# A two-layer attention and mixture-of-experts kernel: scatters in their own turn, last down-projections in half columns, first projections from raw rows, forget sums spread by a DMA

## The chip, the cores and the metric

The kernel runs on one core of one Trainium2 chip. The metric is the device time of one execution in microseconds (us); smaller is better. All data is float32. The engines are named as the profile names them: PE is TensorE's matmul pipe and PEld its weight load, DVE is VectorE, ACT is ScalarE, POOL is GpSimd and SP is SyncE, which here only issues DMAs. A "q" behind an engine's name is its instruction queue.

## The reference

256 tokens of width 1024 pass through two layers and a last norm. Cut to what matters:

```python
for l in range(2):
    h = rmsnorm(x, norm_attn[l])              # x * rsqrt(mean(x^2) + 1e-6) * gain
    proj = h @ w_in[l]                        # 1024 -> 6336: q, k, v of three attentions, gates, merge logits
    out_a = nsa_attention(...)                # 8 heads: compressed, selected and window branches
    c_q, c_kv = rmsnorm(mla_cq, ...), rmsnorm(mla_ckv, ...)
    out_b = causal_block_attention(q_b, k_b, v_b, ...)           # 8 heads with latent keys and values
    log_f = log_sigmoid(fox_f + fox_b_f[l])                      # 8 heads
    cum_log_f = cumsum(log_f, axis=1)                            # over the 256 tokens
    out_c = causal_block_attention(..., cum_log_f)               # score + cum[q] - cum[k]
    mixed = sum of sigmoid(merge + b) * (out @ w_o)              # three branches
    x = x + mixed @ w_out[l]
    t = rmsnorm(x, norm_ffn[l])
    # routing: one group of 4, two experts of its 8; then for each of 32 experts
    a, u = t @ w_gate[e], t @ w_up[e]                            # 1024 -> 256
    x = x + sum_e (silu(a) * u * weight[e]) @ w_down[e]          # 256 -> 1024
return rmsnorm(x, norm_final)
```

The expert weights are 32 x 3 MB in each layer, 201 MB over both. They are read once.

## The kernel before

**Memory.** `ring` is 20 slots of 1 MB in SBUF. In the attention stage slots 4, 5, 6, 7, 0, 1, ... (8 of them, `att_slot`) take the 36 loads of a layer's `w_in`, `w_uq`, `w_o` and `w_out`, and the other 12 MB (`region`) hold activations. In the expert stage all 20 slots take the 96 loads of the experts (`moe_slot`). `tail` holds what lives across both (`kept`). SP issues nearly all loads, in an order written out by hand, each behind a wait for the semaphore that says its slot is free. All engines run their own instruction lists with explicit semaphores.

**Attention stage.** Each of the two rows of 128 tokens is squared and summed (ACT L1037, DVE L1155), POOL works out 1/rms (`norm_pool`), DVE multiplies (L1161), PE turns h into `hT` by 16 transposes (L772), and DVE and ACT take it out of PSUM with the gain (L1166, L1044). In layer 0 PE runs `WARM` = 14 matmuls on the identity (`keep_warm`, L519) once the constants have landed, in layer 1 once the block begins. A float32 matmul is two instructions in the profile, a transpose one.

Then come 13 projections (`JOBS`; L_MPA is the first, L_MPB the second), each 16 matmuls of K = 128 against one 1 MB load: L841 (the first), L781 (`columns`) and L787 (`rows`). Between them lie the compression matmuls (L798), and in layer 0 the setup matmuls of the position bias (L569, L572). The job L_KS is the sixth, L_KW the seventh. After them follow the latent q, k and v (L875 to L892), compressed scores (L900), the transposes of the latent q (L910), and then the sums of the log forget gates: for each of 8 heads a column of `lf` is broadcast to 128 columns and multiplied with a triangle of ones (L930, L932), which leaves cum[k] on all 128 partitions; DVE multiplies by -8 and adds the causal mask into `bias8` and `bias0` (L1328, L1330). `gate_logits(0)` (L781 again) comes next, behind a wait for `s_mqte` 4, the four evictions of the latent q by ACT (L1101), then the compressed branch's output, then 16 units of attention, in which PE, DVE and ACT pass scores, probabilities and transposes to each other, and the merge (L1029).

**Expert stage.** w_out (L1485) adds into x, the tokens are routed, and experts are computed in 8 groups of 4, 32 token places each. In group g PE does: gate and up (L1579 in group 0, `gate_up`, L1557, in the others) behind the waits for its 8 loads; the gather of group g+1 (L1530); the transposes of the hidden rows (L1603), after ACT (L1678) and DVE (L1799, L1804); the scatter of group g-1 (`scatter`, L1564, 4 matmuls of 512 columns) into four PSUM banks; the transposes of the weighted selection (L1618); and the down matmuls (L1629), in two halves n = 0, 1 of 512 columns each, which ACT takes out (L1685). The last group's scatter follows behind the loop, and DVE adds the four banks to x (L1820).

SP's loads of the expert stage follow in `moe_sync`: load c of group g' = (c-20)//12 and place i waits for `s_g0` (group 0's gate and up), for `s_gu` g' (place 0: the slots of gate and up are free) and for `s_y` (place 8: those of down). The last four loads, c = 92 to 95, are the last group's downs, 1 MB each with 8 KB a partition. Behind them SP issues the first four loads of the next layer.

## Time and profile before

| | |
|---|---|
| time, median of 3 runs | 1103.22 us (1102.62 to 1103.24) |
| time of the profiled execution | 1102.17 us |
| its span on the core | 1100.2 us |
| PE busy | 970.0 us (88%), 5879 instructions |
| DVE, ACT, POOL busy | 274.2, 206.4, 24.7 us |
| mean granted TensorE clock | 0.95 |
| moved by DMA | 289.92 MB, mean 264 GB/s |

The span is what the profile covers; the 2.0 us between it and the execution's time lie around it. Busy time is a share of the whole, and the two layers each have a stage that PE fills and one that the weights' transfers fill, so that the mean says little; the rows below are read by stage.

### The profile page before, as it was taken

To read this page: it belongs to the slowest core of one execution; us is meant where nothing else is said; L and a number is where in the kernel's file an instruction comes from. 1 tells how busy PE (TensorE), PEld (TensorE's weight loads), DVE (VectorE), ACT (ScalarE), POOL (GpSimd) and SP (SyncE) were. 2 spreads that over 40 slices of the span, in tenths; PEclk is the share of its full clock that TensorE was granted. 3 is DMA by queue.
4 is the path that set the end of the run, shared out by engine and by line. 5 is a ranking of instruction groups with operands and counts; after the bars stand their busy time and mean duration, and the time that the engine had idled before them with its cause. 6 is when DMAs were issued, how large, how long until landed. Compare 5 with 4: busy or idle time off the path is not lost. (4 is left out here: it accounts for less than half of the span.)

```text
span 1100.2 us, 14272 instructions
## 1 busy us (share of the span) xinstructions
PE 970.0 (88%) x5879; PEld 694.0 (63%) x5879; DVE 274.2 (25%) x950; ACT 206.4 (19%) x561; POOL 24.7 (2%) x68
## 2 busy tenths in 40 slices
PE   7999999999999966777799999999999999666666
PEld 6898678778886333333289877887888854222222
DVE  2210433342423111110021214344333321000102
ACT  1211254441012100000011103444400300000001
POOL 0000000000000000000010000000000000000000
PEclk9999999999999988888899999999999999888888
DMA  9968233436946999999996342443398479999993
GB/s 287 284 152 266 78 103 127 158 111 231 365 169 232 420 422 421 420 422 421 364 251 228 117 152 59 133 136 132 115 332 317 154 309 421 422 420 423 421 422 123
DMA packets 122758, 289.92 MB, mean 264 GB/s; under 512 B 13390, under 2 KB 84164, under 8 KB 100164
## 3 DMA queue, kind: packets, MB, share of 16 engines
q1 hardware_dynamic: 119472, 286.25, 70.0%
q10 hardware_dynamic: 3220, 2.74, 1.5%
q8 instruction: 48, 0.79, 0.3%
q14 instruction: 18, 0.15, 0.0%
HBM read 286.35 MB, written 2.62 MB: 263 GB/s over the span
## 5 line engine op out<-in xcount | busy, mean ns | idle before, releaser
L781 PE MATMUL bank<-tail,ring 128*128 128x256 f32 x1280 | 288.8, 381 | 0.0
L781 PEld LDWEIGHTS bank<-tail,ring 128*128 128x128 f32 x1280 | 239.3, 190 | 38.9 <-issue 8.3
L1557 PE MATMUL bank<-ring,tail 128*32 128x512 f32 x896 | 123.6, 713 | 100.1 <-DMA ring<-in_moe_w_up 100.1
L1557 PEld LDWEIGHTS bank<-ring,tail 128*32 128x32 f32 x896 | 34.4, 128 | 188.9 <-issue 188.9
L1799 DVE SCALAR_TENSOR_TENSOR tail<-tail,bank 128x256 f32<-128x256 f32 x16 | 6.7, 422 | 318.2 <-ACT tail L1678 318.2
L1029 PE MATMUL bank<-tail,ring 128*128 128x256 f32 x384 | 83.4, 380 | 0.0
L1029 PEld LDWEIGHTS bank<-tail,ring 128*128 128x128 f32 x384 | 72.8, 190 | 10.2 <-issue 0.3
L1119 ACT ACTIVATE ring<-ring,small 128x128 f32<-128x128 f32 (+1 forms) x128 | 56.6, 443 | 77.5 <-DVE small L1362 77.5
L1530 PEld LDWEIGHTS bank<-tail 128*128 128x128 f32 x512 | 58.5, 192 | 12.9 <-issue 12.2
L1530 PE MATMUL bank<-tail 128*128 128x128 f32 x512 | 61.9, 278 | 0.8 <-DVE tail L1737 0.5
L1629 PE MATMUL bank<-ring,tail 128*32 128x512 f32 x512 | 58.2, 595 | 0.6 <-DVE tail L1810 0.6
L1564 PE MATMUL bank<-tail 128*128 128x512 f32 x128 | 57.8, 594 | 0.0
L1485 PE MATMUL bank<-ring,tail 128*128 128x256 f32 x256 | 56.7, 380 | 0.0
L787 PE MATMUL bank<-ring,tail 128*128 128x256 f32 (+2 forms) x320 | 53.7, 327 | 0.0
L1485 PEld LDWEIGHTS bank<-ring,tail 128*128 128x128 f32 x256 | 48.2, 190 | 6.3
L787 PEld LDWEIGHTS bank<-ring,tail 128*128 128x128 f32 x320 | 49.7, 191 | 3.6
L1678 ACT ACTIVATE tail<-bank 128x256 f32<-128x256 f32 x16 | 6.1, 384 | 237.9 <-PE bank L1557 214.9
L1355 DVE CUSTOM_DVE_ANT_0 ring<-bank,ring 128x128 f32<-128x128 f32 x96 | 28.6, 354 | 62.7 <-PE bank L971 62.7
L1564 PEld LDWEIGHTS bank<-tail 128*128 128x128 f32 x128 | 23.2, 191 | 24.6 <-issue 24.6
L1629 PEld LDWEIGHTS bank<-ring,tail 128*32 128x32 f32 x512 | 15.0, 109 | 32.1 <-issue 31.1
L971 PE MATMUL bank<-ring 64*128 64x128 f32 (+3 forms) x256 | 34.8, 347 | 0.0
L1377 DVE TENSOR_TENSOR ring<-ring,small 128x256 f32<-128x256 f32 x64 | 32.9, 555 | 1.1
(253 smaller groups left out, 777.2 us busy)
## 6 DMA issues: line engine op xcount, KB each, us to landing
ring<-in_moe_w_gate SPq DMA_DIRECT2D x64, 1024.0 KB, 26.2
ring<-in_moe_w_up SPq DMA_DIRECT2D x64, 1024.0 KB, 26.4
ring<-in_moe_w_down SPq DMA_DIRECT2D x64, 1024.0 KB, 23.3
ring<-in_w_in SPq DMA_DIRECT2D x48, 1024.0 KB, 7.4
ring<-in_w_out SPq DMA_DIRECT2D x8, 1024.0 KB, 10.4
ring<-in_w_o_mla SPq DMA_DIRECT2D x4, 1024.0 KB, 5.1
ring<-in_w_o_fox SPq DMA_DIRECT2D x4, 1024.0 KB, 5.0
ring<-in_w_o_nsa SPq DMA_DIRECT2D x4, 1024.0 KB, 5.4
```

The costliest lines, as they stand in the source:

```text
L781: last = pe.matmul(dst, weight(k), hT[:, k, :], start=(k == 0), stop=(k == KD - 1))
L787: last = pe.matmul(dst, hT[:, k, t * P:(t + 1) * P], weight(k), start=(k == 0), stop=(k == KD - 1))
L971: last = pe.matmul(bank[half][:, lo:hi], q[:, t * P:(t + 1) * P], k[:, 0:hi - lo], start=True, stop=True)
L1029: last = pe.matmul(bank[q % 4][:, 0:T], wo[:, c, (m % 4) * P:(m % 4 + 1) * P], oT[:, b, c, :], start=(c == 0), stop=(c == 3))
L1119: last = act.activation(pr, pr, ACT.Exp, scale=scale, bias=mx[:, c:c + 1], accum_out=sm[:, c:c + 1])
L1355: last = dve.tensor_tensor_reduce(out=prob[u % 3][:, half, lo:hi], in0=bank[half][:, lo:hi], in1=b, scale=1.0, scalar=PAD, op0=ALU.add, op ...
L1377: last = dve.tensor_tensor(pr, pr, bc(factors(rs, u)[:, t, :], [P, 2, hi - lo]), ALU.mult)
L1485: last = pe.matmul(bank[4 + i][:, t * T:(t + 1) * T], mixT[:, k, t * P:(t + 1) * P], w[:, k, :], start=(k == 0), stop=(k == KD - 1))
L1530: last = pe.matmul(b[:, (k % 4) * P:(k % 4 + 1) * P], h2[:, t, k, :], Sel[:, g % 2, t, :], start=(t == 0 and k % 4 == 0), stop=(t == NT - ...
L1557: last = pe.matmul(bank[4][CAP * e:CAP * e + CAP, :].rearrange("p (a f) -> p a f", a=2), XT[:, g % 2, k, CAP * e:CAP * e + CAP], ring[:, l ...
L1564: return pe.matmul(bank[2 * t + half][:, :], ST[:, g % 2, t * P:(t + 1) * P], ysb[:, 512 * half:512 * half + 512], start=(g == 0), stop=(g ...
L1629: last = pe.matmul(bank[5 + n][CAP * e:CAP * e + CAP, :], hidT[:, a, CAP * e:CAP * e + CAP], ring[:, moe_slot(12 * g + 8 + e), a * D + 512 ...
```

## The change

Four parts, in the words of the code:

1. **First projections from raw rows.** PE transposes x itself (not h); the gain goes in on the way out of PSUM (`xT`), the sum of squares comes after it on ACT and DVE. The jobs L_MPA and L_MPB multiply xT, and 1/rms is applied when their result is taken out. Behind L_MPA PE spreads 1/rms over all partitions (two matmuls with the identity into bank 7, `s_rb`), and DVE multiplies xT by it into `hT` (four instructions of 128x512, `s_hn`), for which the job L_NQ waits. The 14 warm-ups of layer 1 go; those of layer 0 run on zeros as soon as they are set. The constants are loaded in two parts, the identity first. The bias matmuls of layer 0 move behind L_MPB.
2. **Forget sums.** Behind L_KS one matmul pair computes the sums of the 8 heads as 8 rows of 256; DVE scales them (`crow`), SP stores them to HBM (8 KB) and, behind load 16, reads them back onto all 128 partitions into `bias8` (1 MB written). DVE adds the mask in two instructions (128x8x128 and 128x8x256) behind `s_kcT`. L930, L932, L1328 and L1330 go.
3. **Own-turn scatter.** Every group scatters behind its own downs. In the last group the transposes of the selection come ahead of those of the hidden rows.
4. **The last downs** are loaded in 8 transfers of 0.5 MB (2 KB rows): the left halves of the four, then the right ones, for which n = 1 waits (`s_late`). In the last group 12 warm-ups (`TAILWARM`) stand ahead of the waits for the last two loads of gate and up.

Some semaphores are merged, and the branch for overflowing experts, which isn't taken here, counts PE's steps in one.

```diff
+TAILWARM = 12
+    def down_half(sp, layer, c, n, done):
+        g, i = divmod(c, 12)
+        src = A["moe_w_down"][layer, 4 * g + GROUP[i][0]].rearrange("(p j) n -> p j n", j=2)
+        slot = ring[:, moe_slot(c), :].rearrange("p (j n) -> p j n", j=2)
+        sp.dma_start(slot[:, :, 512 * n:512 * n + 512], src[:, :, 512 * n:512 * n + 512]).then_inc(done, 16)
...
     def setup_tensor(pe):
+        pe.wait_ge(u_ms, 1)
+        for _ in range(WARM):
+            pe.matmul(bank[7][:, 0:P], zeros, zeros, start=True, stop=True)
+        pe.wait_ge(u_id, 32)
+        pe.transpose(bank[5][:, 0:16], stage[0:16, :], ident[0:16, 0:16]).then_inc(u_prep, 1)
...
                 attention_load(sp, layer, n)
+                if n == RING + L_KW:
+                    sp.wait_ge(s_cr, 1)
+                    sp.dma_start(cum_rows[layer], crow).then_inc(s_cs, 16)
+                if n == RING + L_FQ + 1:
+                    sp.wait_ge(s_cs, 16)
+                    sp.wait_ge(s_hc, 1)
+                    sp.dma_start(bias8, cum_rows[layer].partition_broadcast(P)).then_inc(s_cb, 16)
...
         def attention_tensor(pe):
-            if layer:
-                keep_warm(pe, WARM, bank[7])
-            for t in range(NT):
-                pe.wait_ge(s_h, t + 1)
-                for k in range(KD):
-                    last = pe.transpose(bank[k // 2][...], hA[:, t, k * P:(k + 1) * P], ident)
+            if layer == 0:
+                pe.wait_ge(u_x, 16 * NT)
+            for r in range(4):
+                for j in range(2):
+                    for t in range(NT):
+                        last = pe.transpose(bank[r][:, j * T + t * P:j * T + t * P + P],
+                                            x[:, t, (2 * r + j) * P:(2 * r + j + 1) * P], ident)
+                last.then_inc(s_ht, 1)
...
                     last.then_inc(s_proj, 1)
                     if layer == 0:
-                        setup_bias_tensor(pe)
+                        setup_columns_tensor(pe)
+                    pe.wait_ge(s_rstd, 1)
+                    for t in range(NT):
+                        last = pe.matmul(bank[7][:, t * P:(t + 1) * P], rstd[:, t:t + 1].broadcast_to([P, P]), ident,
+                                         start=True, stop=True)
+                    last.then_inc(s_rb, 1)
                     continue
+                if n == L_NQ:
+                    pe.wait_ge(s_hn, 4)
...
+                if n == L_MPB and layer == 0:
+                    setup_bias_tensor(pe)
+                if n == L_KS:
+                    pe.wait_ge(s_lf, 1)
+                    pe.matmul(bank[7][0:H, 0:T], lf[:, 0, :], cst[:, K_TRI:K_TRI + T], ...)
+                    pe.matmul(bank[7][0:H, P:T], lf[:, 1, :], cst[:, K_TRI:K_TRI + P], ...).then_inc(s_fb, 1)
...
             pe.wait_ge(s_mve, 2)
-            pe.wait_ge(s_lf, 1)
-            for i in range(4):
-                (two heads each: lf column broadcast x triangle, L930 and L932)
             pe.wait_ge(s_mqte, 4)
             gate_logits(0)
...
+            dve.wait_ge(s_rb, 1)
+            for r in range(4):
+                dve.tensor_tensor(hT[:, 2 * r:2 * r + 2, :], xT[:, 2 * r:2 * r + 2, :],
+                                  bank[7][:, 0:T].unsqueeze(1).broadcast_to([P, 2, T]), ALU.mult).then_inc(s_hn, 1)
...
+            dve.wait_ge(s_cb, 16)
+            dve.tensor_tensor(bias0, bias8[:, :, 0:P], mask[:, :, P:T], ALU.add).then_inc(s_fbe, 1)
+            dve.wait_ge(s_fbe, 1)
+            dve.tensor_tensor(bias8, bias8, mask, ALU.add).then_inc(s_fbe, 1)
             take(12, fv[:, :, 256:512], two(bank[0]))
...
+            sp.wait_ge(s_gu, NGRP - 2)
+            for c in range(LOADS - 4, LOADS):
+                down_half(sp, layer, c, 0, landed[moe_slot(c)])
+            for c in range(LOADS - 4, LOADS):
+                down_half(sp, layer, c, 1, s_late)
...
                 for i in range(8):
+                    if g == NGRP - 1 and i == 6:
+                        keep_warm(pe, TAILWARM, bank[5])
                     moe_wait(pe, 12 * g + i)
...
-                if g:
-                    pe.wait_ge(s_ste, g)
-                    pe.wait_ge(s_ye, 2 * g)
-                    for half in range(2):
-                        for t in range(NT):
-                            last = scatter(g - 1, t, half)
-                    last.then_inc(s_scat, 1)
...
+                    if n == 1 and g == NGRP - 1:
+                        pe.wait_ge(s_late, (layer + 1) * 64)
...
+                pe.wait_ge(s_ste, g + 1)
+                for half in range(2):
+                    pe.wait_ge(s_ye, 2 * g + half + 1)
+                    for t in range(NT):
+                        last = scatter(g, t, half)
+                        if g == NGRP - 1:
+                            last.then_inc(s_fin, 1)
+                if g < NGRP - 1:
+                    last.then_inc(s_scat, 1)
```

## Rows read from the trace of the kernel before

**Rows 1.** The page, part 2: DMA in 40 slices of 27.5 us.

```profile
DMA  9968233436946999999996342443398479999993
GB/s 287 284 152 266 78 103 127 158 111 231 365 169 232 420 422 421 420 422 421 364 251 228 117 152 59 133 136 132 115 332 317 154 309 421 422 420 423 421 422 123
```

**Rows 2.** Who PE waited for, whole span: total us, times, longest us.

```profile
PE bank L1557 <- DMA ring<-in_moe_w_up: 100.1, 12, 10.5
```

**Rows 3.** Windows: busy by engine, granted clock, DMA share, GB/s.

```profile
344.00:346.00 2.00, 2.00 (x20) 0.73 (x24) 1.05 (x5) 0.00 (x0) 0.04 (x1) 1.00 0.00 0
...
1078.00:1079.00 1.00, 0.11 (x4) 0.00 (x0) 0.41 (x1) 0.38 (x1) 0.00 (x0) 1.00 0.48 197
```

**Rows 4.** Timeline, first 60 us: start, length, what, [idle before].

```profile
5.80 6.16 PE L519 MATMUL bank<-cst 128*128 128x128 f32 x28 [5.80 <-DMA cst<-in_shape_c]
...
7.31 1.23 DVE L1155 CUSTOM_DVE_ANT_0 ring<-x_res 128x1024 f32<-128x1024 f32 x1 [7.31 <-DMA x_res<-in_x]
...
13.33 1.97 PE L772 MATMUL bank<-cst,ring 128*128 128x128 f32 x16 [1.25 <-DVE ring L1161]
...
15.59 7.15 PE L841 MATMUL bank<-ring,tail 128*128 128x256 f32 x32 [0.30 <-DVE tail L1166]
...
25.00 5.45 PE L787 MATMUL bank<-ring,tail 128*128 128x192 f32 x32
...
30.28 24.34 PE L781 MATMUL bank<-tail,ring 128*128 128x256 f32 x112
```

**Rows 5.** DMA issues at 1.6 us and from 48 to 60: KB, us to landing.

```profile
ring<-in_w_in SPq DMA_DIRECT2D x1, 1024.0 KB, 8.6
...
ring<-in_w_in SPq DMA_DIRECT2D x1, 1024.0 KB, 34.9
```

**Rows 6.** Timeline, start of layer 1.

```profile
552.77 3.39 PE L519 MATMUL bank<-cst 128*128 128x128 f32 x28 [1.62 <-PEq L1823]
...
558.15 7.14 PE L841 MATMUL bank<-ring,tail 128*128 128x256 f32 x32 [0.22 <-DVE tail L1166]
```

**Rows 7.** Timeline, forget sums and the first gate logits, layer 0.

```profile
125.92 1.95 PE L910 MATMUL bank<-cst,ring 128*96 128x128 f32 x16
...
127.80 2.03 ACT L1101 ACTIVATE ring<-bank 96x512 f32<-96x512 f32 x4
...
129.70 0.68 DVE L1328 SCALAR_TENSOR_TENSOR ring<-bank,cst 128x512 f32<-128x512 f32 x1
...
133.49 3.62 PE L781 MATMUL bank<-tail,ring 128*128 128x256 f32 x16
```

**Rows 8.** Part 6 of the page: median us from issue to landing.

```profile
ring<-bias_table SPq DMA_DIRECT2D x2, 1024.0 KB, 5.6
```

**Rows 9.** Timeline, first turns of the expert stage, layer 0, PE and SP.

```profile
359.00 7.05 PE L1557 MATMUL bank<-ring,tail 128*32 128x512 f32 x64
...
366.11 1.76 SPq L499 DMA_DIRECT2D ring<-in_moe_w_down  x4
...
369.89 3.60 PE L1564 MATMUL bank<-tail 128*128 128x512 f32 x8
...
379.54 8.77 PE L1557 MATMUL bank<-ring,tail 128*32 128x512 f32 x64 [2.27 <-DMA ring<-in_moe_w_up]
```

**Rows 10.** Timeline, last group of either layer (528.79: layer 0).

```profile
528.79 9.58 PE L1557 MATMUL bank<-ring,tail 128*32 128x512 f32 x64 [9.46 <-DMA ring<-in_moe_w_up]
...
1068.95 9.15 PE L1557 MATMUL bank<-ring,tail 128*32 128x512 f32 x64 [9.87 <-DMA ring<-in_moe_w_up]
...
1079.52 0.50 PE L1603 MATMUL bank<-cst,tail 128*128 128x128 f32 x2 [1.41 <-DVE tail L1804]
...
1083.60 3.64 PE L1629 MATMUL bank<-ring,tail 128*32 128x512 f32 x32
```

**Rows 11.** Window in the last group of layer 1: TensorE's granted clock rises.

```profile
1073.00:1073.50 0.50, 0.50 (x8) 0.14 (x4) 0.00 (x0) 0.00 (x0) 0.00 (x0) 0.81 0.97 410
```

**Rows 12.** Window of DMA alone, layer 0: expert loads with rows of 2 KB.

```profile
276.00:278.00 2.00, 1.00 1.05 386
```

More of the change, by code:

```diff
@@ L182, in program @@
     hT = kept(0, KD, T)
+    xT = kept(2048, KD, T)
     mixT = kept(2048, KD, T)
@@ L200, in program @@
     hA = region(2048, NT, D)
+    zeros = region(2048, P)
     mqT = region(2048, H, T)
@@ L359, in program @@
     s_fb = csem("cum_forget_psum")
+    s_cr = csem("cum_forget_rows_taken")
+    s_cs = csem("cum_forget_rows_stored")
+    s_cb = csem("cum_forget_spread")
     s_fbe = csem("cum_forget_taken")
@@ L556, in setup_gpsimd @@
         pool.memset(rexp, -0.5)
+        pool.memset(zeros, 0.0).then_inc(u_ms, 1)
         pool.memset(rbd, 0.0)
@@ L1035, in attention_scalar @@
             if layer == 0:
-                act.wait_ge(u_x, 16 * NT)
+                act.wait_ge(u_cols, 1)
+            for r in (1, 3):
+                act.wait_ge(s_ht, r + 1)
+                for j in range(2):
+                    last = act.activation(xT[:, 2 * r + j, :], bank[r][:, j * T:(j + 1) * T], ACT.Copy,
+                                          scale=g_att[:, layer, 2 * r + j:2 * r + j + 1])
+                last.then_inc(s_xTa, 1)
             act.activation(hA[:, 0, :], x[:, 0, :], ACT.Square, accum_out=ss[:, 0:1]).then_inc(s_ss, 1)
@@ L1039, in attention_scalar @@
                 setup_loads(act)
-                act.wait_ge(u_cols, 2)
-            for r in (1, 3):
-                act.wait_ge(s_ht, r + 1)
-                for j in range(2):
-                    last = act.activation(hT[:, 2 * r + j, :], bank[r][:, j * T:(j + 1) * T], ACT.Copy,
-                                          scale=g_att[:, layer, 2 * r + j:2 * r + j + 1])
-                last.then_inc(s_hTa, 1)
             def take(n, dst, src):
@@ L1050, in take @@
                 act.activation(dst, src, ACT.Copy).then_inc(s_eva, 1)
-            take(1, mp[:, :, 256:448], two(bank[1])[:, :, 0:192])
+            act.wait_ge(s_proj, L_MPB + 1)
+            act.wait_ge(s_rstd, 1)
+            for t in range(NT):
+                last = act.activation(mp[:, t, 256:448], two(bank[1])[:, t, 0:192], ACT.Copy, scale=rstd[:, t:t + 1])
+            last.then_inc(s_eva, 1)
             act.wait_ge(s_evd, 1)
@@ L1153, in attention_vector @@
             if layer == 0:
-                dve.wait_ge(u_x, 16 * NT)
+                setup_gains_vector(dve)
+            for r in (0, 2):
+                dve.wait_ge(s_ht, r + 1)
+                dve.tensor_tensor(xT[:, 2 * r:2 * r + 2, :], two(bank[r]),
+                                  bc(g_att[:, layer, 2 * r:2 * r + 2], [P, 2, T]), ALU.mult).then_inc(s_xTd, 1)
             dve.tensor_tensor_reduce(out=hA[:, 1, :], in0=x[:, 1, :], in1=x[:, 1, :], scale=1.0, scalar=0.0,
@@ L1178, in take @@
                 dve.tensor_copy(dst, src).then_inc(s_evd, 1)
-            take(0, mp[:, :, 0:256], two(bank[0]))
+            dve.wait_ge(s_proj, L_MPA + 1)
+            dve.wait_ge(s_rstd, 1)
+            for t in range(NT):
+                last = dve.tensor_scalar(mp[:, t, 0:256], two(bank[0])[:, t, :], rstd[:, t:t + 1], None, ALU.mult)
+            last.then_inc(s_evd, 1)
             take(2, nqT[:, 0:2, :], two(bank[2]))
@@ L1431, in moe_sync @@
             load_overflow(sp)
-            for c in range(SLOTS, LOADS):
+            for c in range(SLOTS, LOADS - 4):
                 g, i = divmod(c - SLOTS, 12)
```

171 lines of the change are left out of this document (78 added, 93 removed).

## The prediction

> **What bounds the kernel now.** I read the page's 40 slices first. DMA's digits [rows 1] show two plateaus of nines, one in each layer's expert stage, with gaps between them. In the list of who PE waited for, one wait is large, 100.1 us in 12 pieces, for the transfers of gate and up [rows 2]; no other wait of PE for data is over 6 us. So there are two regimes. Where the digits are low, PE fills the time, and every us taken off PE's chain moves all that follows. On a plateau the weights' transfers fill it, and PE's work counts only behind the last transfer. The windows show where one turns into the other: at 344 to 346 nothing is moved while PE works without a gap, so the plateau begins when PE frees the first slots; it ends at 1078 to 1079, with the last downs [rows 3]. Its length is 76 MB at one rate and isn't touched. What is saved ahead of it shifts it, what is saved behind it is saved, and what is saved inside is waited away.
>
> **Start of layer 0.** PE's first projection starts at 15.6 [rows 4]. The constants land at 5.8, x at 7.3, and the 1 MB of the first projection's weights 8.6 us after its issue at 1.6, so at 10.2 [rows 4, 5]. In the changed kernel the warm-ups (6.2 us) need only zeros and run from about 1.1 to 7.3; the transposes of x then take 2.0 us, and the first quarter of xT is out of PSUM about 1 us after x is there. So the weights come last, at 10.2: 5.4 us earlier. Behind it PE now has a transpose and the spreading of 1/rms, four instructions of 0.12 us (the pitch of L519 in [rows 6]), 1.0 us with its gaps. The bias matmuls, which hold the gap from 22.7 to 25.0 [rows 4], move behind the second projection and cost the same 2.3 us there. 10.2 + 7.15 + 1.0 + 5.3 + 2.3 = 26.0, against 30.3 for the third projection [rows 4]: **4.3 us** saved. If the weights land as much as 0.8 earlier, since most of the constants now come behind them, it is 5.1; if 0.8 later, 3.5. DVE's four multiplications of 128x512 (0.68 each [rows 7]) are hidden beside the second projection's 5.3 us; without that cover they would cost 2.7.
>
> **Start of layer 1.** PE starts at 552.8 either way, at the block's start. Transposes of x take 1.9 or 2.0 [rows 4], so the first projection starts at 554.7 and not at 558.15 [rows 6]: 3.5. The squares, 1.3 us on each engine, and POOL's rsqrt now have the 7.1 us of that projection as cover. The spreading costs 0.6 here: **2.9 us** saved.
>
> **The clock there.** The 28 warm-up instructions of 3.39 us [rows 6] went at full clock. Without them the stretch from the last scatter (its end is 1.62 us ahead of 552.77 [rows 6]) to 554.7 holds 3.5 us in which PE does transposes only. After an idle time of 2.27 us a gate and up matmul set took 8.77 us where the same set takes 7.05 at full clock [rows 9]; after 9.5 to 9.9 us it took 9.58 and 9.15 [rows 10]. So a fall to half costs 1.7 to 2.5, and no fall costs 0. No row shows whether transposes hold the clock. By length, 3.5 is nearer to the gap of 2.27 that lost it than to the gap of 1.62 that kept it, so I take the fall, **2.1 us** lost. The Trainium skill (TensorE: Matmul & The Clock Gate, Part 4: PE-mode transpose) says that the full rate does not engage for transposes; by that page the loss comes, and if the page doesn't hold here the sum is 2.1 better.
>
> **Forget sums.** The old part starts behind the transposes that end at 127.9, and `gate_logits(0)` comes at 133.5 [rows 7]. Without it PE would go on at once, but that step waits for the fourth eviction by ACT, which ends at 127.80 + 2.03 = 129.83 [rows 7]. So 3.5 are saved and not 5.6, in each layer: **7.0 us**. PE stands idle for 2.0 there; if that drops the clock, it costs 1.7 each [rows 9]. The 8-row form costs PE two instructions of 256 columns (0.22 each, L841 in [rows 4]) and two of 128 (0.12, L519 in [rows 6]) behind L_KS, 0.7 with rounding: **1.3 us** lost over both layers. Its wait for `s_lf` should be free: DVE's last steps for lf hang on the job before, and L_KS gives them some 7 us of PE's work as cover; if lf came that late again, the wait would be PE's. The rest is off the path if the spread lands in time. It is issued behind load 16, at some 80 us, and 1 MB of the same form took 5.6 us from issue to landing [rows 8]; DVE asks for it at about 95 and needs 3.5 us for the mask (0.68 for 512 columns [rows 7]), and the next in its queue, the eviction of the thirteenth job, is due only at 108. On SP the waits for `s_cr` and `s_cs` stand ahead of loads 15 and 17, which the merge gates need after 129.
>
> **Own-turn scatters.** A scatter is 3.6 us of PE [rows 9]. In groups 2 to 6 PE has nearly 10 us of waiting to put it in [rows 2]. In group 0 and 1 it comes ahead of the next gate and up. The loads that wait for group 1's gate and up go out at 366.1 now [rows 9], would go out at 370, and at that time 8 MB issued before last until 377: the queue doesn't run dry. Cost 0; bound from the other side, 3.6 if it did. In the last group the scatter, the selection's transposes and the bubbles lie between 1079.5 and 1083.6 on the path [rows 10]; without them the downs start 1.0 after the transposes of the hidden rows (0.50, then DVE's copy), so 3.1 are saved in each layer: **6.2 us**.
>
> **Warm-ups in the last group.** Its gate and up take 9.58 and 9.15 [rows 10] against 7.05 [rows 9], since PE comes out of an idle time at half clock. The clock rose 4.2 us after work began at 1068.95 [rows 10, 11]. The warm-ups start when six of eight loads are there, 5.0 us ahead of the last (2 MB at 422 GB/s [rows 1]), and 24 instructions of 0.22 [rows 4] last 5.3 at half clock. So they fill the wait, the clock rises about when the last load is there, and I take 7.4 for the set: 2.2 and 1.75, **3.9 us** saved. Bounds: the 28 warm-ups at the program's start went at half clock for all their 6.2 us [rows 4], and if that happens here 0.3 is lost for the overrun and about 1.5 gained each; nothing at all is the floor.
>
> **Half columns.** The last downs used to be there at about 1078.5 [rows 3], and PE asked at 1083.6. Now it asks for the left halves at 1078.3 and for the right ones at 1080.0. The left ones are there 5 us earlier than the right; 2 KB rows moved at 386 GB/s [rows 12] and the plateau's 8 KB rows at 422 [rows 1], so 4.2 MB take 10.9 us and not 9.9, and the right halves land near 1079.5. Cost 0, bound 1.
>
> **Sum.** -4.3 - 2.9 + 2.1 - 7.0 + 1.3 - 6.2 - 3.9 = -20.9. The profiled execution took 1102.2 (span 1100.2 and 2.0 around it) and lies 1.0 under the median of the three runs. 1102.2 - 20.9 = 1081.3, with the 1.0 on top **1082.3**; its own range, from the terms' bounds, is 1080.5 to 1085. Under 0.2% (2.2 us) this kernel's measurement can't be told from no change.
>
> **Rivals.**
> - *The clock holds* through the transposes of layer 1: 1080.2. For it: only 1.62 us are wholly idle [rows 6]. Chance 0.25.
> - *The ends don't shorten as planned*: the clock rises late and the right halves land late. 3.9 and 1.0 come back: 1087.2. For it: the cold start of 6.2 us [rows 4]. Against it: 4.2 us at 1068.95. Chance 0.18.
> - *The first 4.3 us are waited for again.* In layer 0 a load issued at 48 landed 34.9 us later [rows 5], at 82.7, and its job now starts at 93.5 and not 98. The store of the bias table fills DMA then. If the loads slip with it by more than 10 us, PE waits in the tenth to twelfth job: 1086.6. Chance 0.09.
> - *Slower: the spread of the forget sums is late.* The 8 KB store is queued behind that same table store, SP waits for it to land before it issues the spread, and DVE stands behind the spread with the evictions that PE's latent q waits for. The store goes out at about 82; at 34.9 us each [rows 5] the spread lands at 152, and PE, which wants its thirteenth job evicted at 108, waits 48 us: 1130. It decides the sign when the spread lands after 125 in layer 0. Against it: by 80 the table's store has nearly drained, and a table read of the spread's size took 5.6 [rows 8]. The Trainium skill (DMA: Bandwidth & Descriptors, the section on why a DMA increments its semaphore by 16) says that a transfer with 8 rows outermost runs on 8 engines at most; by that page the new 8-row store and the table's store, which also has 8 outermost, share their engines. The 34.9 us [rows 5] agree with such a jam, but no row of them shows which engines it holds. Chance 0.03.
>
> **Chances.** The forecast has 0.43, the rivals 0.25, 0.18, 0.09 and 0.03; 0.02 is left for more than all this. 1078 to 1088 takes in all but the slow case and some of the unknown. Faster 0.96, same 0.01, slower 0.03.
>
> **What would show it.** In the changed kernel's profile: the first projection at 10 and its successor L_NQ at 26; in layer 1 the first projection 1.9 us behind the block's first transpose, with a granted clock of 0.5 in part of it if the fall is right; PE idle for 2 us ahead of the first gate logits and nothing there from L_KS's four instructions; the plateau of layer 0 starting at about 337 and not 347; in the last groups a gate and up set of 7.4 us and downs 2.4 us behind its end. A wait of PE on DVE in the thirteenth job, of DVE on the spread, or a DMA share under 0.9 inside a plateau would each make it wrong.

## Result and the profile after

The changed kernel takes **1090.88 us** (median of 4 runs, 1086.04 to 1092.14) and the kernel before 1102.92 (4 runs, 1102.22 to 1103.24): ratio 0.9889, 95% interval 0.9874 to 0.9905. It is faster by 12 us where 20.9 were forecast, and lies 8.6 us above the forecast and 2.9 outside its range. The same kernel, run again beside the first experiments, took 1087.69 (1087.25 to 1091.72), ratio 0.9878 [0.9865, 0.9892]: 14.4 us faster than the kernel before, and just inside the range. The profiled execution took 1092.14, span 1090.3, the longest of the four.

The page of the changed kernel, part 2 in 40 slices of 27.3 us (PE clock in tenths, DMA in tenths, GB/s):

```profile
PEclk9999999999999998888899999999999999888888
DMA  9879333436945999999997542443398479999994
GB/s 301 198 173 346 96 104 129 156 115 215 368 188 191 422 422 421 420 421 422 367 314 237 166 143 78 138 144 117 105 348 308 154 309 422 421 421 420 422 415 158
```

The two plateaus are still there [rows 1]. Timeline of PE in layer 0, from the first projection to the first gate logits (start, length, what, idle time before):

```profile
9.29 7.17 PE L879 MATMUL bank<-ring,tail 128*128 128x256 f32 x32 [0.96 <-DMA ring<-in_w_in]
...
24.48 24.42 PE L819 MATMUL bank<-tail,ring 128*128 128x256 f32 x112
...
52.40 0.60 PE L909 MATMUL bank<-cst,small 128*8 128x256 f32 x2
...
75.67 15.77 PE L819 MATMUL bank<-tail,ring 128*128 128x256 f32 x64 [3.34 <-DMA ring<-in_w_in]
...
98.63 13.98 PE L825 MATMUL bank<-ring,tail 128*128 128x256 f32 x64
...
126.24 1.95 PE L962 MATMUL bank<-cst,ring 128*96 128x128 f32 x16
130.24 5.38 PE L819 MATMUL bank<-tail,ring 128*128 128x256 f32 x16 [2.05 <-issue]
```

The third projection starts at 24.48 and not at 30.28 [rows 4]: 5.8 us gained. At 75.67 PE waits 3.34 us for a load, and the set behind it takes 15.77 us, 14.08 at full clock (77.04 in the kernel before). At 126.24 the transposes of the latent queries start 0.3 us *later* than before [rows 7]. So the whole start of layer 0 is lost by then. The first gate logits follow behind 2.05 us of idle time, at half clock: 5.38 us, 3.62 before [rows 7].

Why a load is late stands in the queues. SP and ACT in the kernel before, then in the changed one:

```profile
42.99 33.60 SPq L462 DMA_DIRECT2D ring<-in_w_in  x5
...
45.17 0.79 ACTq L629 DMA_DIRECT2D bias_table<-ring  x1
```

```profile
39.45 0.80 ACTq L660 DMA_DIRECT2D bias_table<-ring  x1
...
42.00 5.21 SPq L724 DMA_DIRECT2D tail<-in_moe_w_router  x1
47.25 31.26 SPq L471 DMA_DIRECT2D ring<-in_w_in  x5
```

The store of the bias table used to go out 2.2 us behind the first of SP's five loads; it comes 5.7 us earlier with the whole start, while SP's small loads ahead of `w_in` come only about 1 us earlier, and so it is now ahead of the five. Issues of the five loads, two of them in the kernel before (at 42.99 and 45.85) and the first in the changed one (KB, us to landing):

```profile
ring<-in_w_in SPq DMA_DIRECT2D x1, 1024.0 KB, 8.3
...
ring<-in_w_in SPq DMA_DIRECT2D x1, 1024.0 KB, 33.6
```

```profile
ring<-in_w_in SPq DMA_DIRECT2D x1, 1024.0 KB, 28.4
```

So the store held up loads in the kernel before as well: SP took 33.6 us to issue the five, and the third landed at 79.4. But the first, for which the ninth projection waits, had landed at 51.3, and the others were not yet wanted. Behind the store the first one lands at 75.6.

Layer 1's start, the last groups of both layers (528.8 and 1069 in [rows 10]), PE:

```profile
524.20 5.46 PE L535 MATMUL bank<-cst 128*128 128x128 f32 x24 [4.32 <-DMA ring<-in_moe_w_up]
529.59 7.23 PE L1608 MATMUL bank<-ring,tail 128*32 128x512 f32 x64
...
539.26 3.64 PE L1676 MATMUL bank<-ring,tail 128*32 128x512 f32 x32 [0.52 <-DVE tail L1861]
542.83 3.70 PE L1615 MATMUL bank<-tail 128*128 128x512 f32 x8
548.16 1.97 PE L811 MATMUL bank<-cst,x_res 128*128 128x128 f32 x16 [1.63 <-PEq L1874]
549.96 7.07 PE L879 MATMUL bank<-ring,tail 128*128 128x256 f32 x32
...
1062.37 7.08 PE L1608 MATMUL bank<-ring,tail 128*32 128x512 f32 x64
...
1071.89 5.34 PE L1676 MATMUL bank<-ring,tail 128*32 128x512 f32 x32 [0.52 <-DVE tail L1861]
1077.16 3.70 PE L1615 MATMUL bank<-tail 128*128 128x512 f32 x8
```

The downs start 2.4 us behind the end of gate and up in both layers, as forecast; in layer 1 they run at half clock (5.34 us for 3.64). In layer 1 the first projection takes 7.07 us: the clock did not fall in the transposes (granted clock 1.00 from 546 to 550).

The first gather in the routing, PE in layer 0, in the kernel before and in the changed one:

```profile
337.29 2.02 PE L1530 MATMUL bank<-tail 128*128 128x128 f32 x16 [0.15 <-ACT tail L1662]
```

```profile
335.81 3.45 PE L1579 MATMUL bank<-tail 128*128 128x128 f32 x16
```

It runs at a granted clock of 0.50 from 336 to 338, and in layer 1 it takes 3.24 us. A wait for VectorE behind it (0.64 us before) takes up part of this, so that it costs some 0.5 us in each layer.

**Where the spans differ.** Each stage ends where the next begins: the first gate and up (343.95 before), the last load of gate and up, the end of its matmuls, the end of the last scatters. The last load lands 4.93 us behind the start of the warm-ups (in the mended kernel's trace 516.18 to 521.11, where PE still waits behind them), so at 529.1 and 1061.9 here. In us against the kernel before; the last column is an experiment's (f1):

| stage | forecast | changed | mended (f1) |
|---|---|---|---|
| attention and routing, layer 0 | -7.15 | -1.0 | -7.9 |
| plateau, layer 0 (184.8 us) | 0 | +1.3 | +0.2 |
| last gate and up (9.58) | -2.2 | -1.9 | -2.5 |
| last downs and scatters (12.8) | -3.1 | -3.1 | -3.1 |
| attention and routing, layer 1 | -3.65 | -3.6 | -5.8 |
| plateau, layer 1 (185.0) | 0 | +1.2 | 0 |
| last gate and up (9.15) | -1.75 | -1.6 | -2.1 |
| last downs and scatters (12.8) | -3.1 | -1.4 | -3.1 |
| end | 0 | +0.1 | 0 |
| sum | -20.9 | -9.9 | -24.1 |

Of the 11.0 us between forecast and changed kernel some 4.0 were lost ahead of the transposes at 126.24, 3.4 in the gate logits of both layers, 1.0 in the gathers, 2.5 in the plateaus, 1.7 in layer 1's last downs and 0.5 at the last gate and up; some 2.4 came back at layer 1's start.

### The profile page after: what moved, and what is told of

It is laid out like the page before. It is cut to its first block and busy times, and to the rows that moved or that the text cites. A ratio compares the mean times of both kernels' runs of the same rounds, so it can differ in the third digit from the quotient of the medians.

```text
span 1090.3 us, 14225 instructions
## 1 busy us (share of the span) xinstructions
PE 975.8 (89%) x5852; PEld 696.0 (64%) x5852; DVE 277.1 (25%) x947; ACT 207.3 (19%) x564; POOL 24.8 (2%) x69
## 5 line engine op out<-in xcount | busy, mean ns | idle before, releaser
L819 PE MATMUL bank<-tail,ring 128*128 128x256 f32 x1280 | 294.3, 386 | 7.4 <-issue 4.1
L819 PEld LDWEIGHTS bank<-tail,ring 128*128 128x128 f32 x1280 | 242.8, 193 | 48.8 <-issue 13.3
L1608 PE MATMUL bank<-ring,tail 128*32 128x512 f32 x896 | 117.4, 683 | 71.7 <-DMA ring<-in_moe_w_up 71.7
L1068 PE MATMUL bank<-tail,ring 128*128 128x256 f32 x384 | 83.4, 380 | 0.0
L1068 PEld LDWEIGHTS bank<-tail,ring 128*128 128x128 f32 x384 | 72.8, 190 | 10.2 <-issue 0.3
L1579 PEld LDWEIGHTS bank<-tail 128*128 128x128 f32 x512 | 61.2, 199 | 12.6 <-issue 11.9
L1579 PE MATMUL bank<-tail 128*128 128x128 f32 x512 | 64.5, 286 | 0.5 <-DVE tail L1788 0.5
L1676 PE MATMUL bank<-ring,tail 128*32 128x512 f32 x512 | 59.9, 610 | 5.2 <-DVE tail L1861 5.2
L1615 PEld LDWEIGHTS bank<-tail 128*128 128x128 f32 x128 | 23.0, 189 | 36.4 <-issue 36.4
```

Of the source, the lines that this page charges most:

```text
L819: last = pe.matmul(dst, weight(k), hT[:, k, :], start=(k == 0), stop=(k == KD - 1))
L1068: last = pe.matmul(bank[q % 4][:, 0:T], wo[:, c, (m % 4) * P:(m % 4 + 1) * P], oT[:, b, c, :], start=(c == 0), stop=(c == 3))
L1579: last = pe.matmul(b[:, (k % 4) * P:(k % 4 + 1) * P], h2[:, t, k, :], Sel[:, g % 2, t, :], start=(t == 0 and k % 4 == 0), stop=(t == NT - ...
L1608: last = pe.matmul(bank[4][CAP * e:CAP * e + CAP, :].rearrange("p (a f) -> p a f", a=2), XT[:, g % 2, k, CAP * e:CAP * e + CAP], ring[:, l ...
L1615: return pe.matmul(bank[2 * t + half][:, :], ST[:, g % 2, t * P:(t + 1) * P], ysb[:, 512 * half:512 * half + 512], start=(g == 0), stop=(g ...
L1676: last = pe.matmul(bank[5 + n][CAP * e:CAP * e + CAP, :], hidT[:, a, CAP * e:CAP * e + CAP], ring[:, moe_slot(12 * g + 8 + e), a * D + 512 ...
```

## The experiments

Medians are of 4 to 6 runs, each kernel timed beside the kernel before (1101.3 to 1102.1). "The unchanged one" is the changed kernel as it is, at 1087.69. It was timed with the result (1090.88) and with the runs whose names begin with e, not with those of f, g and h; its nine runs together have a median of 1088.9. A difference between a kernel of f, g or h and 1087.69 is therefore uncertain by some 3 us, and counts as shown only where rows of the traces bear it out.

> The changed kernel once more, beside the others of its batch. Its four runs so far lay between 1086.0 and 1092.1, median 1090.9. If the spread comes from where the clock falls, runs with a higher mean granted clock are the shorter ones, and the median stays at 1088 to 1092. If it came from the chip of the first batch, all runs lie close together at another level.

Measured: 1087.69.

**The late load.** The store is moved on ACT's queue behind the eighth take.

```diff
-        act.wait_ge(u_cp, 1)          # in setup_trig_scalar
-        act.dma_start(table, tabs.unsqueeze(1).broadcast_to([H, P, OH_W])).then_inc(u_tb, 16)
+            if layer == 0:            # in attention_scalar, behind take(7, ...)
+                act.wait_ge(u_cp, 1)
+                act.dma_start(table, tabs.unsqueeze(1).broadcast_to([H, P, OH_W])).then_inc(u_tb, 16)
```

> The changed kernel with the store of the bias table moved on ACT from its place behind the log forget gates (39.5 us) to behind the seventh projection's eviction (about 67 us). Theory A (the store, now issued 5.7 us earlier, goes ahead of the projections' loads 8 to 12 and takes back the start's gain in layer 0): PE does not wait for w_in at 75.7, the last projection ends about 5 us earlier, the time falls by 4 to 5.5 us. Rival (the loads are late for their own sake, because DMA is full at the start whatever ACT stores): the wait of 3.3 us at the ninth projection stays and the time moves by less than 1 us. If the new 8 KB store or the spread now meets the table's store, DVE waits for the spread longer than the 1.9 us of the changed kernel.

Measured: 1083.04 (1081.04 to 1085.7), ratio 0.9822 [0.981, 0.9835], 4.65 less. Windows from 44 to 52 us of the changed kernel and of this one (busy of each engine, clock, DMA share, GB/s):

```profile
44.00:52.00 8.00, 8.00 (x53) 7.43 (x52) 2.13 (x7) 0.00 (x0) 0.00 (x0) 1.00 0.51 74
```

```profile
44.00:52.00 8.00, 8.00 (x52) 7.38 (x51) 2.13 (x7) 0.00 (x0) 0.72 (x1) 1.00 1.04 326
```

With the store in the queue half of the DMA time is used and 74 GB/s moved; without it 326. Its timeline (PE, SP, DVE):

```profile
72.55 14.08 PE L817 MATMUL bank<-tail,ring 128*128 128x256 f32 x64
...
109.76 7.09 PE L926 MATMUL bank<-ring 128*128 128x384 f32 x16 [1.96 <-DVE ring L1222]
...
80.24 5.24 SPq L743 DMA_DIRECT2D ring<-cum_rows  x1
...
105.46 1.22 DVE L1324 TENSOR_TENSOR ring<-ring,cst 128x1024 f32<-128x1024 f32 x1 [10.05 <-DMA ring<-cum_rows]
```

The wait and the cold set are gone, and the first gate and up of layer 0 starts at 339.45, 4.0 us earlier than in the unchanged kernel of the same set of runs (343.44). But the store now stands ahead of the spread of the forget sums: VectorE waits 10.05 us for it and PE 1.96 us for VectorE, and then works at half clock. This is the slow rival of the prediction in small.

**Why the store holds the queue.** The same 1.5 MB, but 128 rows outermost instead of 8, by way of a 12 KB copy to HBM. That changes two more things: the source is now HBM and no longer 8 partitions of SBUF, and the store goes out at 42.66, 0.4 us behind the first of the five loads, not at 39.45.

```diff
-        act.dma_start(table, tabs.unsqueeze(1).broadcast_to([H, P, OH_W])).then_inc(u_tb, 16)
+        act.dma_start(rows8, tabs).then_inc(u_t8, 16)
...
+        act.wait_ge(u_t8, 16)         # behind the angles
+        act.dma_start(table.rearrange("h p w -> p h w"), rows8.unsqueeze(0).broadcast_to([P, H, OH_W])).then_inc(u_tb, 16)
```

> The changed kernel with the table's store in two steps from the same place: the eight rows first as 12 KB, then the 1.5 MB from there with 128 rows outermost instead of 8. If the store is slow because eight rows outermost keep it on half of the engines, it now lasts some 5 to 10 us instead of 30, SP's five loads behind it are issued in about 9 us as with the late store, TensorE waits for nothing at the ninth projection, and the time is that of the late store or a little less: 1083, 1081.5 to 1084.5. If it is the store itself, whatever its shape, the loads land as late as before and the time stays at 1087.7, within 1.

Measured: 1080.29 (1078.3 to 1083.03), ratio 0.9806 [0.9793, 0.9819]. Its timeline of SP, PE and DVE, then a window and the DMA issue (KB, us to landing):

```profile
42.29 14.29 SPq L473 DMA_DIRECT2D ring<-in_w_in  x5
...
72.81 14.08 PE L823 MATMUL bank<-tail,ring 128*128 128x256 f32 x64
...
95.59 1.22 DVE L1327 TENSOR_TENSOR ring<-ring,cst 128x1024 f32<-128x1024 f32 x1
```

```profile
44.00:52.00 8.00, 8.00 (x51) 7.35 (x50) 2.13 (x7) 0.00 (x0) 0.72 (x1) 1.00 1.01 304
...
bias_table<-bias_rows ACTq DMA_DIRECT2D x1, 1536.0 KB, 10.4
```

The store lands in 10.4 us, the five loads go out in 14.3 us and not 31.3, and neither PE at 72.8 nor VectorE at 95.6 waits. So it is not a matter of 1.5 MB being stored there. Nor is it the place: in the kernel before the narrow store went out 2.2 us behind the first load, and the five still took 33.6 us to issue. What is left is the shape and the source together; no run changes one alone. The Trainium skill (DMA: Bandwidth & Descriptors, the section on why a DMA increments its semaphore by 16) says that a transfer with 8 rows outermost runs on at most 8 of the 16 engines; the share of 0.51 with 8 rows and of 1.01 with 128 agree with it. Which engines these are no view shows. But half of the engines is not all. The store's queue from 74 to 79 us in the run with the late store, where next to nothing else was moved, and from 43 to 53 with the wide store (packets, MB, share of 16 engines):

```profile
q10 hardware_dynamic: 167, 0.26, 44.5%
```

```profile
q10 hardware_dynamic: 1040, 1.57, 47.6%
```

A packet of 1.5 KB took 213 ns of one engine's time there and 73 here (0.445 x 5 us x 16 / 167, and 0.476 x 10 us x 16 / 1040). So the narrow store was slow by a factor of 2 from the engines that it left idle and of 2.9 from the time of each packet, and the second factor, for which the source is a candidate, stays unexplained.

**The gap of the forget sums.**

```diff
             pe.wait_ge(s_mve, 2)
+            keep_warm(pe, 8, bank[4])
             pe.wait_ge(s_mqte, 4)
```

> The changed kernel with 8 warm-up matmuls (16 instructions) in the gap where the forget sums were, ahead of the wait for the latent q's evictions. Theory B (the 2.05 us of idle PE let the clock fall, and the first gate logits take 5.4 us and not 3.6 in both layers): the logits take 3.6 us, the time falls by 3 to 3.6 us. Rival (the clock falls there by chance, and the run-to-run spread hides it): under 1.5 us on the median.

Measured: 1084.11 (1082.34 to 1085.57), ratio 0.9832 [0.982, 0.9845], 3.6 less. The logits run at full clock in both layers; layer 0:

```profile
129.52 1.95 PE L535 MATMUL bank<-cst 128*128 128x128 f32 x16
131.69 3.72 PE L819 MATMUL bank<-tail,ring 128*128 128x256 f32 x16 [0.22 <-ACT ring L1144]
```

In the unchanged kernel's trace of the same set of runs only one of the two logits was at half clock (1.7 us). The rest of the 3.6 lies elsewhere: both its gathers were at half clock and here none is, and its plateau and last gate and up of layer 1 are longer. That the filler is worth 3.6 is not shown.

**The parts undone, one by one.** First the forget sums as before: the four loops of sixteen matmuls behind the wait for `s_mve`, their eight evictions on VectorE, no rows of eight, no store, no spread.

> The changed kernel with the forget sums as before: sixteen matmuls behind the latent query transposes, taken by VectorE with the mask, no rows of eight, no store, no spread. What the part brings is then the difference to the unchanged one (1087.7). The forecast's size: 7.0 less 1.3 is 5.7 us, 1093.4. By the traces since: 3.5 us in each layer, less 0.75 each for the rows of eight, less 1.7 in the layers where the gate logits run at half clock behind the 2.05 us gap (one of two in that profile): 3.8 us, 1091.5, between 1090 and 1092.5. That the part brings nothing (the rival): 1087.7.

Measured: 1090.99 (1090.21 to 1091.69), ratio 0.9904 [0.9889, 0.992]: 3.3 over 1087.69, but the same as the unchanged one's first median, so that the medians alone say anything from 0 to 3.3. The rows say more. Attention and routing of layer 1 take 329.6 us with the old sums and 327.1 with the new ones where nothing falls to half clock (e1), so the part brings 2.5 us in a layer; in the changed kernel's profile, with logits and gather at half clock, it is 329.2, and next to nothing is left.

Then the scatter order of before (`scatter(g - 1, t, half)` behind the hidden transposes, the last group's at the end; one wait for `s_ye` ahead of the warm-ups, which keeps their bank free).

> The changed kernel with the scatter of a group behind the next group's gate and up, and that of the last group at the end, as before; halves and warm-ups stay. The forecast's size of the own-turn scatter, 3.1 us in each layer: 1087.7 + 6.2 = 1093.9, between 1092.5 and 1095. The rival: the old order leaves TensorE no stops in the last group (the scatters stand where it now waits 1.05 and 0.52 us), the downs are never at half clock, and the part is worth less, 4 to 5 us: 1092.

Measured: 1093.85 (1089.67 to 1097.84), ratio 0.9929 [0.9908, 0.995]: 6.2 over 1087.69, as the forecast had it, and by the rows 3.07 in each layer (from the end of the last gate and up to the end of the scatters 12.77 us here and 9.70 with the own turn). Its plateaus are as long as the mended kernel's (start of the first gate and up to the last load: 185.1 and 185.0 for 185.0 and 185.0), so the own-turn order costs nothing inside.

Whole downs instead of halves (the four loads back in the loop, no `s_late`):

> The last group's four down matrices are loaded whole again, with no second wait. The forecast's step (the halves cost and bring nothing, bound 1 us): 1087.7, within 0.7. The rival: the own-turn scatter brings the last downs forward to 9.7 us behind the start of the last gate and up, while four whole loads of 1 MB take some 10 us at 410 GB/s behind the last up; then the downs wait 0.5 to 2 us in each layer without the halves, and the time is 1089 to 1091.

Measured: 1089.54 (1088.46 to 1090.64), ratio 0.9885 [0.987, 0.99], which overlaps the unchanged one's. In its profile the downs wait 0.56 and 0.52 us for VectorE and never for a load. So the halves bring nothing that this measurement shows.

**The warm-ups.** `TAILWARM = 0` and `TAILWARM = 8`:

> The changed kernel without the 12 warm-ups of the last groups. Theory C (the warm-ups begin 3.7 us ahead of the last load, last 5.46 us, so they hold the set up for 1.7 us and win about 2.1 by the clock: little is left): the set starts 1.7 us earlier in each layer and takes 8.7 to 9.6 us; the time rises by 0 to 2 us. Forecast's theory (they win 2 us in each layer): the time rises by 3.5 to 4 us. If they cost more than they bring, it falls.

Measured: 1093.82 (1090.6 to 1097.35), ratio 0.9928 [0.9912, 0.9945], 6.1 more. Its last gate and up of layer 0:

```profile
529.90 8.47 PE L1608 MATMUL bank<-ring,tail 128*32 128x512 f32 x64 [8.32 <-DMA ring<-in_moe_w_up]
```

In layer 1 they take 8.41. From the landing of the last load to the end of gate and up it is 8.7 us in both layers, and 7.8 and 7.6 in the changed kernel's profile, 7.2 and 8.0 in the unchanged one's of this set: the stage shows 2.0 to 2.2 us over both layers, which is about what theory C gives. The median shows 6.1. So the runs do not settle theory C, and what lies between 2.2 and 6.1 is not shown to be the warm-ups'.

> TAILWARM = 8 alone. Theory C2: the twelve warm-ups start on a cold engine and last 5.46 us, 1.7 us longer than the 3.7 us that are left to the last load, and so eat the gain that they bring; eight last some 3.4 us, the last gate and up start when the load lands and take about 7.1 us: 1 to 1.5 us less in each layer, 1085.5 us (1084.5 to 1086.5). The rival, that eight are too few: the gate and up take some 8.4 us again as without warm-ups, and the time lies between 1088.5 and 1094.

Measured: 1090.23 (1087.45 to 1093.68), ratio 0.9887 [0.9868, 0.9906]: no better than 1087.69. In layer 0 they leave a stop of 1.72 us and gate and up take 9.98 us:

```profile
524.18 3.21 PE L535 MATMUL bank<-cst 128*128 128x128 f32 x16 [3.48 <-DMA ring<-in_moe_w_up]
529.11 9.98 PE L1608 MATMUL bank<-ring,tail 128*32 128x512 f32 x64 [1.72 <-issue]
```

The last load lands 4.93 us behind the start of the warm-ups, so the wait to be filled is 4.9 us and not the 3.7 that this expectation had; twelve that start at half clock overrun it by 0.5 us.

> Four warm-ups behind the last group's selection transposes, where TensorE waits 1.05 us for VectorE's hidden rows. Theory: the downs of the last group ran at half clock (5.34 us for 3.64) in layer 1 of two profiles out of four because of the two short stops of 1.05 and 0.52 us ahead of them; filled, they are never cold, and the median falls by 0.5 to 1.5 us: 1086.5. The rival: it was the warm-ups' own overrun or chance, and nothing moves: 1087.7 within 0.7.

Measured: 1087.04 (1084.61 to 1088.89), ratio 0.9864 [0.9849, 0.9879]. Its downs take 3.64 and 3.65 us, but the median cannot be told from the unchanged one's.

**All together:** the late store, the gap filled, `TAILWARM = 8`, and on VectorE the two additions of the mask behind the last take.

```diff
-            dve.wait_ge(s_cb, 16)
-            dve.tensor_tensor(bias0, bias8[:, :, 0:P], mask[:, :, P:T], ALU.add).then_inc(s_fbe, 1)
...
             take(12, fv[:, :, 256:512], two(bank[0]))
+            dve.wait_ge(s_cb, 16)
+            dve.tensor_tensor(bias0, bias8[:, :, 0:P], mask[:, :, P:T], ALU.add).then_inc(s_fbe, 1)
...
```

> Four edits together on the changed kernel: the table's store behind the eighth take of ScalarE; eight warm-ups of TensorE in the 2.0 us gap that the forget sums leave; the two additions of the mask on VectorE behind its last take, so that they no longer stand in front of it when the spread lands late (in the run with the late store alone VectorE waited 10.05 us for the spread and TensorE 1.96 us for VectorE); and eight warm-ups instead of twelve ahead of the last gate and up. If the losses are separate, as the runs so far say, the gains add: 4.6 + 3.6 + 1.1, and 0.5 to 2 for the shorter warm-ups, from 1087.7: 1077.5 us, between 1075.5 and 1079.5. The rival: what one edit fills lets the clock fall elsewhere (the routing's gather, the last downs), and the sum stops near 1081.

Measured: **1077.92** (1077.13 to 1083.69), ratio 0.9787 [0.9764, 0.981], 9.8 under the unchanged one and 24 under the kernel before. Its timeline of PE:

```profile
72.68 14.08 PE L817 MATMUL bank<-tail,ring 128*128 128x256 f32 x64
...
108.81 5.40 PE L926 MATMUL bank<-ring 128*128 128x384 f32 x16 [0.88 <-DVE ring L1223]
...
125.53 3.72 PE L817 MATMUL bank<-tail,ring 128*128 128x256 f32 x16 [0.22 <-ACT ring L1145]
...
336.09 7.07 PE L1632 MATMUL bank<-ring,tail 128*32 128x512 f32 x64 [0.62 <-DVE tail L1837]
```

All three losses of layer 0 are gone, and its first gate and up starts 7.9 us earlier than in the kernel before. The medians' gains, 4.65 and 3.6, leave 1.5 for the other two edits, but this sum does not say which edit brought what: from the late store alone to this kernel the first logits move from 128.22 to 125.53, both at full clock, so the mask's place brings 2.7 us by itself.

> The mended kernel (late store, gap filled, mask behind the last take) with twelve warm-ups instead of eight ahead of the last gate and up. In the mended kernel's profile the eight begin 3.9 us ahead of the last load and leave a stop of 1.3 us behind them, and gate and up run at full clock, 7.07 us. Alone, eight gave 1090.2 for the twelve's 1087.7. If twelve fill the stop and start at full clock (4.5 us) they overrun by nothing or 0.7 us: 1077 to 1079.5, no difference from the 1077.9 of the eight. If the twelve start on a cold engine (5.46 us) they overrun by 1.6 us in each layer: 1080 to 1081.

Measured: 1078.95 (1078.28 to 1081.23), ratio 0.9798 [0.9783, 0.9812]. The medians of eight and twelve can't be told apart. The profiles can: with twelve the last gate and up take 7.07 to 7.44 us in all 20 places of the ten profiles that have them; eight leave a stop of 1.2 to 1.7 us, and in three of eight places gate and up then start cold (9.98 above, 9.22 and 9.17 in h2 and h3). Twelve are the safer choice.

> The mended kernel with no warm-ups ahead of the last gate and up. By the rows of the run without warm-ups (8.4 us for 7.07 in each layer) they bring 2.7 us: 1080.6. By that run's median (6.1 us over the unchanged one) they bring more than their own matmuls: 1083 to 1084.5. By the forecast's size, 3.9: 1081.8.

Measured: 1085.58 (1084.24 to 1085.9), ratio 0.9854 [0.9839, 0.9869], 7.7 more. Its last gate and up, where the mended kernel takes 7.07 twice:

```profile
521.11 9.46 PE L1610 MATMUL bank<-ring,tail 128*32 128x512 f32 x64 [9.02 <-DMA ring<-in_moe_w_up]
...
1054.14 9.19 PE L1610 MATMUL bank<-ring,tail 128*32 128x512 f32 x64 [9.27 <-DMA ring<-in_moe_w_up]
```

These two rows are 4.5 us of the 6.4 between the two profiles' spans. Another 1.2 are a longer plateau in layer 1, and 0.6 lie in its attention and routing, where a gather ran at half clock; both lie ahead of that layer's warm-ups. So between these two profiles the warm-ups are worth some 4.5 us, a little over the forecast's 3.9 and twice what the run without them alone showed, and what the two medians show beyond that is not shown to be theirs.

> The wide store, the gap filled and eight warm-ups in the last groups, but no edit to the mask's place, since nothing delays the spread then. With the theory of the engines it equals the mended kernel, 1078, within 1. If the store's shape is not the cause, it is the run with the gap filled alone, 1084.

Measured: 1082.8 (1079.12 to 1083.39), ratio 0.9809 [0.9793, 0.9825]: it can't be told from the wide store alone, and 1078 was expected. The logits are at full clock as meant, but in this profile three gathers (3.02, 3.58 and 3.37 us for 2.02, 2.05 and 2.02) and the last gate and up of layer 1 (9.22) are not. In the wide store's own profile the gap was unfilled, and the clock held in both layers.

> The mended kernel once more, on the chip of this call: 1077.9, within 1.5.

Measured: 1080.13 (1078.53 to 1081.09), ratio 0.9795 [0.9782, 0.9809]. Both times the mended kernel lies under every median of the kernel before and of the changed one; the wide store alone (0.9806) can't be told from it. Here its last gate and up of layer 0 start cold:

```profile
521.00 9.17 PE L1610 MATMUL bank<-ring,tail 128*32 128x512 f32 x64 [1.20 <-issue]
```

## Why the prediction was wrong

- **Start of layer 0** failed. At the third projection 5.8 us had come where 4.3 were forecast; at the ninth 5.0 went, 3.34 in the wait and 1.7 at half clock, and the rows of eight took 0.75. That is the rival "The first 4.3 us are waited for again", which had 0.09 and nearly the right price, but placed the wait in the tenth to twelfth job and had the loads slip by some 10 us. Its row was at hand, 34.9 us from issue to landing [rows 5], and the prediction took it for a delay that all the loads have. What decides is which loads stand behind the store: in the kernel before the first of the five, the ninth projection's, was ahead of it and landed at 51.3; in the changed one it is behind it and lands at 75.6. The store passed it because the earlier start pulled ACT's issue forward by 5.7 us and SP's by about 1; that step was costed for PE alone, not for what ACT issues with it. The late store gave back 4.65 by the median. By the start of layer 0's first gate and up it is 4.0: 5.0 at the load and 1.7 by gate logits that stayed at full clock, less 2.7 lost at the spread. The wide store has this start at 336.24, 7.2 earlier, of which 2.2 are logits and a gather that stayed at full clock.
- **Forget sums** were mis-sized: 5.7 forecast; by the rows 5.1 where no clock falls (2.5 in a layer, g1 beside e1), and each fall takes 1.7 from it. At 9 falls in 18 places that is an estimate of 3.4, and g1's median gave 0 to 3.3. The 2.0 us gap lies where it was put (2.05), and the clause "if that drops the clock, it costs 1.7 each" should have been in the sum with its chance: the logits took 5.38 us and not 3.7 in 9 of 18 places of this kind, over the nine profiles that have the gap and no filler. The rows of eight cost 0.75 each for 0.65.
- **The clock there** failed in the other direction. In all 16 profiles with the new start, the changed kernel's and the experiments', layer 1's first projection takes 7.07 us behind a stop of 1.59 to 1.64. The Trainium skill (TensorE: Matmul & The Clock Gate, Part 4: PE-mode transpose), by which the full rate does not engage for transposes, does not hold for this stretch; the measurement decides. The start of layer 1 gained 3.2 where 2.9 less 2.1 were forecast.
- **Own-turn scatters** were right: -3.1 in layer 0's last group, and 3.07 in each by g2's rows; nothing was lost inside the plateaus. What was not foreseen is that the downs, now behind two short stops of 1.05 and 0.52 us, can run at half clock: +1.7 in layer 1 of this profile, and in 4 of the 28 places of the profiles that have both stops unfilled. Nor were the routing's gathers: the first one is at half clock in 20 of 32 layers of the new profiles and in neither of the kernel before, some 0.5 us each; what lets its clock fall is open.
- **Warm-ups** were right in the mechanism, and nearly in size against the kernel before: 1.9 and 1.6 in the changed kernel for 2.2 and 1.75; up to 2.5 and 2.1 where they start at full clock. Against the same kernel without them it is 2.0 to 2.2 in one pair of profiles (e3) and 4.5 in another (g4).
- **Half columns**: nothing, as said.
- **The slow rival** did not happen in the changed kernel (VectorE waits 1.9 us for the spread, off the path), but the late store called it up: 10.05 us. It needed the table's store ahead of the spread (67.69 and 80.24).
- Not foreseen at all: a plateau of 186.1 and 186.2 us for 184.8 and 185.0, 2.5 us. Part of it goes in the first 12 us, where the windows of the changed kernel show

```profile
347.00:355.00 8.00, 7.70 (x72) 5.00 (x65) 2.43 (x5) 0.77 (x2) 0.57 (x2) 1.00 0.99 390
880.00:888.00 8.00, 7.70 (x72) 5.13 (x68) 2.67 (x6) 0.77 (x2) 0.76 (x2) 1.00 1.00 408
```

against 420 and 419 GB/s in the same place of the kernel before, at the same DMA share: 8 us x 30 / 421 = 0.6 us and 0.2 us. Both layers of e1 and f3 have it too, and no layer of e2, f1, g1, g2 and g3. The same kernel's second profile (e0) has a plateau as short as before in layer 0 and a long one in layer 1, so it differs between executions of one kernel, and is not shown to come from the change. Its cause stays open.

Open too is where the clock falls from run to run. The changed kernel's runs spread over 6 us, those of before over 1 to 3, and two profiles of it differ in such places (the logits of layer 1 took 5.36 us in one and 3.69 in the other, its last downs 5.34 and 3.74). With the gap filled h2 shows falls elsewhere and f1 none; no run here settles which stop lets go of the clock.

## What to carry to other kernels

When a stage is pulled forward, list every DMA that its engines issue and ask what it now stands ahead of; two queues whose order flips can take back the whole gain. Look for loads that are already late without being waited for: they show what the slow transfer does before it costs anything. Look at the form of such a transfer before its place: a store of the same bytes with 128 rows outermost, from HBM, was as good as all moves of the narrow one. An idle time that an edit leaves on TensorE is to be costed with the matmuls behind it at half clock, at the share of places where that happened (here half), or filled. A median of one set of runs is not to be set against that of another without its rows: the same kernel's two medians lie 3.2 us apart.

## What the hardware showed

A 1.5 MB store from 8 partitions, with 8 rows outermost, cut the traffic of all queues to 74 GB/s at a DMA share of 0.51 in the window from 44 to 52 us, and its packets took 213 ns each; from HBM and with 128 rows outermost it landed in 10.4 us, the window's share was 1.01, and a packet took 73 ns. The same 2.05 us of idle time was followed by matmuls at 1.2 GHz in 9 of 18 places and at 2.4 GHz in the others. In one profile (f3) even 3.34 us kept the clock. And a stop of 1.6 us with 1.97 us of transposes behind it did not cost the clock in any of 16 profiles.
